# Weighted sum of past value pages: TensorE per page, or ScalarE and VectorE with one TensorE sum per sample

## What is computed

```python
BATCH, SEQ, DEC_BATCH, DEC_SEQ = 1, 256, 8, 1
PAST_LEN, PAGE_SIZE, A_HEADS, A_DH = 1024, 128, 8, 128
...
    v_past = cache_v[l][page_table].reshape(DB, past_len, A_HEADS, A_DH)
...
        p = jax.nn.softmax(logits, axis=-1)
        p_sel = p[..., :n_sel * MOBA_BLOCK].reshape(B, H, qc, n_sel, MOBA_BLOCK)
        p_own = p[..., n_sel * MOBA_BLOCK:]
        o = (jnp.einsum('bhqsj,bhqsjd->bqhd', p_sel, vs)
             + jnp.einsum('bhqj,bhjd->bqhd', p_own, v_own))
...
    merged = (g_a * (oa.reshape(B, S, A_W) @ lw['w_br_moba']).astype(jnp.float32)
              + g_r * (o_r.reshape(B, S, R_VW).astype(x.dtype) @ lw['w_br_ret']).astype(jnp.float32)
              + g_m * (om.reshape(B, S, M_W).astype(x.dtype) @ lw['w_br_mem']).astype(jnp.float32))
    x = x + merged.astype(x.dtype) @ lw['w_out']
```

## Time and profile before

| what | value |
|---|---|
| time, median of 3 runs | 2693.95 us (2692.69 to 2694.89) |
| span of the profiled execution | 2688.8 us |
| TensorE matmuls busy | 2662.4 us, 99% of the span |
| TensorE weight loads busy | 2590.7 us, 96% |
| VectorE busy | 1541.8 us, 57% |
| ScalarE busy | 1092.0 us, 41% |
| GpSimd busy | 147.5 us, 5% |
| mean granted clock of TensorE, 1 is full | 0.997 |

### The profile page before, as it was taken

How to read it: one execution, slowest core, us unless ns; L and a number is a source line. 1 busy time by engine, 2 the same in 40 slices (tenths; PEclk the granted TensorE clock), 3 DMA queues, 4 the chain that set the end, 5 groups by cost and what they waited for, 6 DMA issues and landing times.

```text
span 2688.8 us, 50855 instructions
## 1 busy us (share of the span) xinstructions
PE 2662.4 (99%) x21748; PEld 2590.7 (96%) x21748; DVE 1541.8 (57%) x2442; ACT 1092.0 (41%) x985; POOL 147.5 (5%) x266
## 2 busy tenths in 40 slices
...
GB/s 267 235 210 186 176 185 182 177 187 177 185 168 175 237 306 299 240 354 392 339 274 334 280 317 320 232 211 198 173 188 175 185 184 177 185 176 186 181 159 115
DMA packets 487449, 600.08 MB, mean 223 GB/s; under 512 B 12608, under 2 KB 447008, under 8 KB 485984
## 3 DMA queue, kind: packets, MB, share of 16 engines
...
...
## 4 chain that ended last, share of the span: by engine, by line
PE 96%; DVE 1%; DMA 1%; ACT 1%; issue 1%; DVEq 0%; POOLq 0%; SPq 0%; ACTq 0%
PE PS L554 30%; PE PS L555 29%; PE PS L556 29%; PE PS L1997 1%; PE PS L590 1%; PE PS L592 1%; PE PS L591 1%; DVE splitL L509 1%; DMA raw<-w_gate 1%; ACT splitH L503 1%; PE PS L1760 0%; PE PS L1497 0%; PE PS L1728 0%; PE PS L1242 0%; PE PS L1356 0%
## 5 line engine op out<-in xcount | busy, mean ns | idle before, releaser
L509 DVE TENSOR_TENSOR splitL<-raw,splitH 128x2048 fp32r<-128x2048 f32 (+1 forms) x462 | 1007.5, 2181 | 841.8 <-ACT splitH L503 840.9
L503 ACT ACTIVATE splitH<-raw 128x2048 fp32r<-128x2048 f32 (+1 forms) x462 | 844.4, 1829 | 1493.4 <-PE PS L556 1443.4
L554 PE MATMUL PS<-gH,splitH 128*128 128x264 f32 x3072 | 880.9, 287 | 5.3 <-DVE splitL L509 5.3
L555 PE MATMUL PS<-gL,splitH 128*128 128x264 f32 x3072 | 871.2, 284 | 0.0
L556 PE MATMUL PS<-gH,splitL 128*128 128x264 f32 x3072 | 870.6, 283 | 0.0
L554 PEld LDWEIGHTS PS<-gH,splitH 128*128 128x128 f32 x3072 | 579.3, 189 | 25.0 <-issue 22.9
L555 PEld LDWEIGHTS PS<-gL,splitH 128*128 128x128 f32 x3072 | 579.7, 189 | 0.5 <-issue 0.2
L556 PEld LDWEIGHTS PS<-gH,splitL 128*128 128x128 f32 x3072 | 576.7, 188 | 0.0
L554 PE MATMUL PS<-hH,splitH 128*128 128x264 f32 x1536 | 436.1, 284 | 0.1
L555 PE MATMUL PS<-hL,splitH 128*128 128x264 f32 x1536 | 435.1, 283 | 0.0
L556 PE MATMUL PS<-hH,splitL 128*128 128x264 f32 x1536 | 434.9, 283 | 0.0
...
## 6 DMA issues: line engine op xcount, KB each, us to landing
...
```

The costliest lines, as they stand in the source:

```text
L503: nc.scalar.activation(splitH[:, s, tiles, :], raw[:, u, 0:nk, :], ACT.Copy).then_inc(hi_ready, 1)
L509: nc.vector.tensor_tensor(splitL[:, s, tiles, :], raw[:, u, 0:nk, :], splitH[:, s, tiles, :].bitcast(F32), ALU.subtract).then_inc(split_re ...
L554: nc.tensor.matmul(out, w_hi, H[:, k, 0:n], start=first, stop=False)
L555: nc.tensor.matmul(out, w_hi, L[:, k, 0:n], start=False, stop=False)
```

## The change

The samples 2 and 5 stay with `pe_value_page`. They go in pairs of pages behind the units of `PE_PAIR_AT`. For the samples 0, 1, 3, 4, 6 and 7 a new tile `vAcc` (128 x 1024) gathers the weighted pages:

- `act_vec_page`: ScalarE multiplies the even pages 0, 2, 4, 6 with the probabilities, 8 instructions of 128 x 128, one for each head. Page 0 goes into `vAcc`, the others are scaled in their ring slot.
- `dve_vec_page`: VectorE does the odd pages 1, 3, 5, 7 (8 instructions of 128 x 128 that multiply and add to `vAcc`) and adds the scaled even pages 2, 4, 6 to `vAcc`, one instruction of 128 x 1024 each.
- `pe_value_sum`: TensorE adds up the partitions of `vAcc`, four matmuls with a matrix of ones. These are in the slots 114, 120, 126, 131, 136 and 140 (samples 0, 1, 3, 4, 6, 7).

`VEC_PAGE_AT` gives the slots of the 48 pages. ScalarE's page 0 of the next sample waits for `v_sum`, the sum of the one before, since there is one `vAcc`. The row of a sum is copied in the same slot (`act_row_copy` from bank 7) and turned two slots later or more: in slots 116, 122, 125, 128, 133, 137, 138 and 142. `dve_decode_out` of this branch moves from slot 141 to 143. The semaphores of the three branches become one that counts, `branch_done`; unit 144 waits for its third count.

```diff
@@ -234,6 +234,7 @@
+    vAcc = at("vAcc", [BR_W], M_QB + 4608)
...
-    def act_row_copy(act, n):
+    def act_row_copy(act, n, bank=4, c0=0):
 
         if n == 0:
             act.wait_ge(st_sent[0], 32)
             act.wait_ge(st_sent[1], 32)
         if n >= 2:
             act.wait_ge(row_turned, n - 1)
-        nc.scalar.activation(row_tile(n)[:, n % 2, :, :], two(PS[:, 4, 0:2 * P]), ACT.Copy).then_inc(row_sb, 1)
+        nc.scalar.activation(row_tile(n)[:, n % 2, :, :], two(PS[:, bank, c0:c0 + 2 * P]), ACT.Copy).then_inc(row_sb, 1)
...
-    VALUES = [("V", k, g) for k in range(DEC) for g in range(NPAGES)]
-    VALUE_AT = {**{T: (3, 2, 1, 2)[T % 4] for T in range(108, 132)}, **{T: 2 for T in range(132, 140)}}
-    assert sum(VALUE_AT.values()) == len(VALUES)
+    PE_SAMPLES, VEC_SAMPLES = (2, 5), (0, 1, 3, 4, 6, 7)
+    PE_PAIR_AT = (112, 116, 119, 123, 126, 130, 132, 135)
+    VEC_PAGE_AT = (108, 108, 109, 109, 111, 112, 112, 113, 113, 114, 115, 116, 117, 117, 118, 119, 120, 120, 121, 121, 123, 124, 124, 125, 125, 126, 127, 128, 129, 129, 130, 130, 131, 131, 132, 132, 133, 134, 134, 135, 135, 136, 136, 137, 138, 138, 139, 139)
+    PE_PAIRS = {T: (PE_SAMPLES[i // 4], 2 * (i % 4)) for i, T in enumerate(PE_PAIR_AT)}
+    VEC_PAGES = {}
+    for i, T in enumerate(VEC_PAGE_AT):
+        VEC_PAGES.setdefault(T, []).append((VEC_SAMPLES[i // NPAGES], i % NPAGES))
+    assert len(PE_PAIR_AT) == 4 * len(PE_SAMPLES) and len(VEC_PAGE_AT) == NPAGES * len(VEC_SAMPLES)
+    SUM_AT = {VEC_PAGE_AT[NPAGES * i + NPAGES - 1] + 1: k for i, k in enumerate(VEC_SAMPLES)}
+    ROWS_MADE = sorted([(PE_PAIR_AT[4 * i + 3], 0, k) for i, k in enumerate(PE_SAMPLES)]
+                       + [(T, 1, k) for T, k in SUM_AT.items()])
+    ROW_NO = {k: n for n, (_, _, k) in enumerate(ROWS_MADE)}
+    ROW_TURN_AT = {}
+    for T, _, k in ROWS_MADE:
+        T = max([T + 2] + [t + 1 for t in ROW_TURN_AT])
+        while T in SUM_AT:
+            T += 1
+        ROW_TURN_AT[T] = k
+
+    def past_rows(Ts, T):
+
+        return PAST_ROWS + sum(t < T for t in Ts)
...
-        v = 0
-        for T in sorted(VALUE_AT):
-            for _ in range(VALUE_AT[T]):
-                at_slot.append((T, 0, VALUES[v]))
-                v += 1
+        for T, (k, g0) in PE_PAIRS.items():
+            at_slot += [(T, 0, ("V", k, g)) for g in (g0, g0 + 1)]
+        for T, pages in VEC_PAGES.items():
+            at_slot += [(T, 1, ("V", k, g)) for k, g in pages]
...
+    def rows_before(samples, k):
+
+        i = samples.index(k)
+        return PAST_ROWS + (ROW_NO[samples[i - 1]] + 1 if i else 0)
+
+    def act_vec_page(act, k, g):
+
+        s = page_there(act, ("V", k, g))
+        i = VEC_SAMPLES.index(k)
+        if i == 0 and g == 0:
+            act.wait_ge(d_prob, 2)
+        if i and g == 0:
+            act.wait_ge(v_sum, i)
+        for h in range(A_HEADS):
+            page = ring[:, s, h * P:(h + 1) * P]
+            last = nc.scalar.activation(vAcc[:, h * P:(h + 1) * P] if g == 0 else page, page, ACT.Copy,
+                                        scale=DA["L"][:, k, g, h:h + 1])
+        if g == 0:
+            last.then_inc(page_used[s], 1)
+        else:
+            last.then_inc(v_prod, 1)
+
+    def dve_vec_page(dve, k, g):
+
+        page_read(dve, ("V", k, g - 1))
+        s = PAGE_NO["V", k, g] % RING
+        if g % 2 == 0:
+            dve.wait_ge(v_prod, 3 * VEC_SAMPLES.index(k) + g // 2)
+            nc.vector.tensor_tensor(vAcc[:, :], vAcc[:, :], ring[:, s, :], ALU.add).then_inc(page_used[s], 1)
+            return
+        page_there(dve, ("V", k, g))
+        if g == 1:
+            dve.wait_ge(d_prob, 2)
+        for h in range(A_HEADS):
+            acc = vAcc[:, h * P:(h + 1) * P]
+            last = nc.vector.scalar_tensor_tensor(acc, ring[:, s, h * P:(h + 1) * P], DA["L"][:, k, g, h:h + 1], acc,
+                                                  ALU.mult, ALU.add)
+        last.then_inc(page_used[s], 1)
+
+    def pe_value_sum(pe, T, k):
+
+        page_read(pe, ("V", k, NPAGES - 1))
+        pe.wait_ge(row_out, past_rows(ROW_TURN_AT, T))
+        for j in range(4):
+            last = nc.tensor.matmul(PS[32 * j:32 * j + A_HEADS, 7, 2 * P:4 * P], ones[:, 0:A_HEADS],
+                                    vAcc[:, 2 * j * P:2 * (j + 1) * P], start=True, stop=True)
+        last.then_inc(v_sum, 1)
+
     def pe_value_page(pe, k, g):
 
         if g == 0:
             pe.wait_ge(d_prob, 2)
-            pe.wait_ge(row_sb, PAST_ROWS + k)
+            pe.wait_ge(row_sb, rows_before(PE_SAMPLES, k))
         s = page_there(pe, ("V", k, g))
         for j in range(4):
             last = nc.tensor.matmul(PS[32 * j:32 * j + A_HEADS, 4, 0:2 * P], DA["L"][:, k, g, :],
                                     ring[:, s, 2 * j * P:2 * (j + 1) * P], start=g == 0, stop=g == NPAGES - 1)
         last.then_inc(page_used[s], 1)
 
...
         if T in (T_GATE + 2, T_GATE + 32 + 2, T_PROJ):
-            pe.wait_ge((r_all_done, m_done, a_done)[(T - T_GATE) // 32], 1)
+            pe.wait_ge(branch_done, (T - T_GATE) // 32 + 1)
...
-        for _ in range(VALUE_AT.get(T, 0)):
-            k, g = values // NPAGES, values % NPAGES
-            if g == 0 and k:
-                pe_row_turn(pe, PAST_ROWS + k - 1)
-            pe_value_page(pe, k, g)
-            values += 1
-        if T == 140:
-            pe_row_turn(pe, PAST_ROWS + DEC - 1)
-        return values
+        if T in ROW_TURN_AT:
+            pe.wait_ge(row_sb, past_rows([t for t, _, _ in ROWS_MADE], T))
+            pe_row_turn(pe, PAST_ROWS + ROW_NO[ROW_TURN_AT[T]])
+        if T in SUM_AT:
+            pe_value_sum(pe, T, SUM_AT[T])
+        if T in PE_PAIRS:
+            k, g0 = PE_PAIRS[T]
+            pe_value_page(pe, k, g0)
+            pe_value_page(pe, k, g0 + 1)
...
-        for _ in range(VALUE_AT.get(T, 0)):
-            k, g = values // NPAGES, values % NPAGES
-            if g == NPAGES - 1:
-                page_read(act, ("V", k, g))
-                act_row_copy(act, PAST_ROWS + k)
-            values += 1
-        return values
+        for k, g in VEC_PAGES.get(T, ()):
+            if g % 2 == 0:
+                act_vec_page(act, k, g)
+        if T in PE_PAIRS:
+            k, g0 = PE_PAIRS[T]
+            if g0 == NPAGES - 2:
+                page_read(act, ("V", k, NPAGES - 1))
+                act_row_copy(act, PAST_ROWS + ROW_NO[k])
+        if T in SUM_AT:
+            k = SUM_AT[T]
+            act.wait_ge(v_sum, VEC_SAMPLES.index(k) + 1)
+            act_row_copy(act, PAST_ROWS + ROW_NO[k], 7, 2 * P)
...
-        for _ in range(VALUE_AT.get(T, 0)):
-            k, g = values // NPAGES, values % NPAGES
-            if g == 0 and k:
-                dve_past_row_out(dve, k - 1, DA["oS"])
-            values += 1
-        if T == 140:
-            dve_past_row_out(dve, DEC - 1, DA["oS"])
-        if T == 141:
+        for k, g in VEC_PAGES.get(T, ()):
+            if g:
+                dve_vec_page(dve, k, g)
+        if T in ROW_TURN_AT:
+            dve_past_row_out(dve, ROW_TURN_AT[T], DA["oS"])
+        if T == 143:
             dve.wait_ge(row_out, PAST_ROWS + DEC)
-            dve_decode_out(dve, link, DKA, a_done)
+            dve_decode_out(dve, link, DKA)
...
```

More of the change, by code:

```diff
@@ L325, in build @@
     page_used = [sem(f"page_used{s}") for s in range(RING)]
+    v_prod, v_sum = sem("v_prod"), sem("v_sum")
     qb_in = [sem(f"qb_in{s}") for s in range(3)]
-    gate_ps, sum_ps, d_sb, d_exp, d_max, d_maxall, d_logit, d_prob, m_done, a_done = map(sem, (
-        "gate_ps", "sum_ps", "d_sb", "d_exp", "d_max", "d_maxall", "d_logit", "d_prob", "m_done", "a_done"))
+    gate_ps, sum_ps, d_sb, d_exp, d_max, d_maxall, d_logit, d_prob, branch_done = map(sem, (
+        "gate_ps", "sum_ps", "d_sb", "d_exp", "d_max", "d_maxall", "d_logit", "d_prob", "branch_done"))
     row_zero, row_sb, row_turned, row_out = map(sem, ("row_zero", "row_sb", "row_turned", "row_out"))
@@ L1542, in dve_past_row_out @@
     def dve_past_row_out(dve, k, out):
-        dve.wait_ge(row_turned, PAST_ROWS + k + 1)
+        dve.wait_ge(row_turned, PAST_ROWS + ROW_NO[k] + 1)
         for et in range(2):
@@ L1999, in pe_value_page, with dve_decode_out @@
         last.then_inc(page_used[s], 1)
-    def dve_decode_out(dve, link, K, done):
+    def dve_decode_out(dve, link, K):
         t = K.t
@@ L2119, in chunk_at, with pe_side @@
         return 42 + 9 * i // 8
-    def pe_side(pe, T, values):
+    def pe_side(pe, T):
         if T == 0:
@@ L2213, in act_evac, with act_side @@
             copy_evac(act, T)
-    def act_side(act, T, values):
+    def act_side(act, T):
         if T == 0:
@@ L2283, in dve_evac, with dve_side @@
             scaled_evac(dve, qaT, rinv[:, :])(B, c, u // 2)
-    def dve_side(dve, link, T, keys, values):
+    def dve_side(dve, link, T, keys):
         if T == 0:
@@ L2341, in dve_side @@
             dve.wait_ge(row_out, PAST_ROWS)
-            dve_decode_out(dve, link, DKM, m_done)
```

(5 more changed lines are left out.)

17 lines of the change are left out of this document (7 added, 10 removed).

## The result

The changed kernel takes 2698.86 us (median of 15 runs, 2695.74 to 2704.31), the kernel before 2694.89 in the same comparison (15 runs). The ratio is 1.0018, 95% interval 1.0011 to 1.0025. It lies just inside the 0.2% that the prediction set as no change, and outside zero: a small loss of 4 us. Forecast were 2696.5 in a range of 2684 to 2708. One thing said ahead of the prediction is set right by the record: in every run since, the time is 1.6 to 1.7 us above the span of the same execution (2703.58 and 2701.9 here). Of the 4 to 6 us given there, the rest is that the profiled execution of before was a short one. The prediction added 5.1 us to get from that execution to a median, and for that the figure holds.

What follows compares the result with a forecast made beforehand. TensorE, filled for 2662.4 of 2688.8 us, was the bound. Saving -19.6, waits 4.0, 6.5, 6.8 and 1.5, clock 3.4 sum to +2.6: 2691.4 profiled, 5.1 more for the median, 2696.5 us; range 2684 to 2708.

Steps and rivals of the forecast that it cites:

- The saving: TensorE's work taken off by dropping 48 value pages and some slot extras, less six sums: 19.6 us, between 18.0 and 22.
- the extra of 0.32 us: TensorE's cost for each slot with any pages, beside 0.43 a page; said to go in five slots, 1.6 us.
- the measure of the prediction: On TensorE, time from a unit's last matmul to the next unit's second, less two steps, taken as the pages' cost.
- (a) Unit 144: TensorE's unit 144 waits for the decode output's five steps, behind VectorE's split for unit 145: 4.0 us, 3.8 to 4.3.
- (b) Page 0: ScalarE's page 0 waits for a sum and delays the next split; units 116, 128, 138 wait 3.2, 2.3, 1.0: 6.5 us.
- (c) The sums: Sums wait for page 7: slot 140 2.6, slot 131 2.9 (page 7's load late), slot 120 1.3; 6.8 us, 3 to 10.
- (d) The small waits: Splits for units 112 and 120 and a page in slot 126 come late: 1.5 us, between 0 and 3.
- The clock: TensorE's granted clock falls after the waits of 4.0 and 3.2 us, 1.7 us each: 3.4 us, 1.7 to 6.8.
- Late pages: Slower rival: ring slots return late, landings of 9.4 us delay pages in slots 126, 131, 138: +8.0, 2704.5 us; chance 0.20.
- The rule of the Trainium skill: Slower rival: GpSimd's page issues held up by VectorE's two-input instructions, about 5 us reaching TensorE: 2701.5 us; chance 0.04.
- Four falls: Slower rival: 2.3 us waits also drop the clock, at unit 128 and sums in 131, 140: +3.4, 2700.0 us; chance 0.09.
- Cheap pages: Faster rival: pages cost 1.7 us on ScalarE and VectorE and land in 3.5: -5.9, 2688.0 us; chance 0.17.

Runs made afterwards that it cites:

- the last kernel: Changed kernel with decode output in slot 142, pages, pairs and sums moved to other slots, VectorE copying turned rows ahead of pages: 2671.65 us, ratio 0.9909.
- The separate run: The kernel before with only its decode output moved from slot 141 to 143: 2699.22 us, ratio 1.0020.
- the second profile: The changed kernel run again unaltered against the kernel before, for another profile: 2699.37 us, ratio 1.0015.
- the wide pages: Changed kernel with one 128x1024 instruction per weighted page in place of eight of 128x128, output wrong, for time alone: 2681.16 us, ratio 0.9948.

## Why the prediction came out right, term by term

**The saving was undersized, 23.3 and not 19.6 us.** The step that failed is the count of the extra of 0.32 us: I had it gone in five slots only, "but most of the others keep the extra for the prompt's attention". It is the pages' own. Before, unit 109's last matmul, the prompt's scores, two pages, and the next unit:

```profile
1541.69 0.28 PE L556 MATMUL PS<-gH,splitL 128*128 128x264 f32 x1
1541.81 0.82 PE L1728 MATMUL PS<-kaR,qaR 128*128 128x128 f32 x4
1542.56 1.05 PE L1997 MATMUL PS<-ring,A_L 128*8 128x256 f32 x16
1543.54 0.39 PE L554 MATMUL PS<-omH,splitH 128*128 128x264 f32 x1
1543.76 0.28 PE L555 MATMUL PS<-omL,splitH 128*128 128x264 f32 x1
```

and in the last kernel the same with scores and no pages:

```profile
1544.06 0.28 PE L557 MATMUL PS<-gH,splitL 128*128 128x264 f32 x1
1544.18 0.82 PE L1749 MATMUL PS<-kaR,qaR 128*128 128x128 f32 x4
1544.65 0.47 PE L555 MATMUL PS<-omH,splitH 128*128 128x264 f32 x1
1544.96 0.28 PE L556 MATMUL PS<-omL,splitH 128*128 128x264 f32 x1
```

From the last matmul of the unit to the second of the next, the measure of the prediction, are 2.07 us with two pages and 0.90 without: two pages cost 1.17 beside a step of the attention, as much as without one (1.18), and not 0.86. In slot 118, with one page, the same two traces give 1.65 and 0.89, so 0.76 for a page and its extra. Of 32 slots with pages 14 groups of pages or sums are left, so 18 x 0.32 = 5.8 us go, not 1.6. That makes 23.8 by the prediction's own sum, and 23.3 were measured, above the 22 that I had put as its end.

**(a) Unit 144: right.** 4.0 forecast, 3.70 in every trace that has it. The separate run shows that it costs the kernel before 4.9 us with its clock.

**(b) Page 0: right in kind, too large.** Unit 116 3.06 (3.2 forecast). Unit 128 had 0.70 (2.3) where a page ahead of it in slot 126 had waited 1.32 us for its transfer (none and 2.30 in the second profile), and unit 138 had none (1.0) behind a turn in slot 137 that had waited 1.32. What TensorE has waited for already, a split is early for. The waits of the turns (1.32 and 1.38) I had not seen: they come from the order on ScalarE and VectorE, where copies of rows stand behind pages.

**(c) The sums: right.** 1.19, 2.19 and 2.90 against 1.3, 2.9 and 2.6. In slot 131 the reason was the other one: page 7 follows at once on the addition of page 6, no transfer holds it.

**(d) The small waits: too small.** Units 112, 120 and 124 and the pages in 126 and 132 wait 1.66, 0.96, 0.48, 1.32 and 0.71, 5.1 us, outside the 0 to 3 that I gave. With the turns it is 7.8 where 1.5 stood.

**The clock: undersized.** Two falls were forecast at 1.7 each; there were three and four, at 1.4 to 2.7.

**The sum.** -23.3 + 21.6 + 8.1 = +6.4 in one execution and -23.3 + 21.1 + 6.9 = +4.7 in the other, +4.0 in the medians, where -19.6 + 18.8 + 3.4 = +2.6 stood. The forecast was right in its main claim, that the saving is real and the order gives it back, and the time came out near by luck as well: a saving too small by 4 met waits and clock too small by 6 to 7.

**The rivals.** Late pages: landings went from 5.6 to 6.1 in the middle, GpSimd's issues stayed at 530 ns (533 before), TensorE waited 2.0 us for transfers in all, and the wide pages leave no room for it:

```profile
L1671 POOL DMA_DIRECT2D ring<-cache_v x64 | 33.9, 530 | 185.6 <-issue 177.7 <-PE PS L2065 6.5 <-DVE vAcc L2038 0.8
...
DMA to landing us min/median/max: 3.8/6.1/8.8
```

The rule of the Trainium skill, "GPSIMD Engine Reference", section 1, on interfaces to the memory that GpSimd shares with VectorE, showed in no issue here: with 210 more instructions of VectorE that have two inputs there, an issue of a transfer takes 530 ns. What it says of GpSimd's own reads and writes no run here shows. Four falls: this rival can't be told from the forecast by the time, and its 2700.0 is as near to the measured 2698.86 as 2696.5 is. The second profile has four, behind the sums in slots 131 and 140 as it said, but behind the page in slot 126 and not behind units 116 and 128; the first has three. Cheap pages: 2.45 and 2.19 us, not 1.7; had they been cheap, 2681 shows what would have come. It is 7 us under the 2688 that I gave for that case, again by the saving.

## What to carry over

Work taken off the bound engine is worth what it costs there only if nothing that releases that engine is queued behind the work's new place. Here the same work gave +4 us or -23.5 us by the slots and the order alone: a copy of 0.2 us, a page ahead of a split, five steps of 0.2 us, and sums too close behind their last page: on the two engines that take over, put what the bound engine waits for ahead of what it doesn't, and let a sum lie one unit behind its last input. And count the extra of a group of small matmuls by itself, with rows of a slot that has only the other group.

## What the runs showed of the clock

In the ten traces of kernels whose stretch has waits of 1.9 us or more, TensorE's granted clock went to half behind all five waits of 3.70 us, all six of 2.90, three of the four of 3.06 to 3.12, two of the seven of 2.19, and the one of 1.96 and the one of 2.30; behind none of 1.76 or less. In the two profiles of the changed kernel, the 3.06 us wait had a fall in one and none in the other, and the 2.19 us wait the reverse. So a single profile says what such a wait costs only within 2 us, and medians of many runs are needed: I had counted falls as if a wait of a given length had one or none. The falls also differ in length: from 8 to 22 of the units' matmuls start 0.22 us apart where they otherwise start 0.12 apart, and with the slow records of a sum or page ahead of them a fall costs 1.4 to 2.7 us. Behind the 3.70 us wait, eight groups of three matmuls take 5.28 us instead of 2.9 in two profiles; in the other three 15 matmuls are slow. Why one is longer than another, these runs don't show.
